# Delta-rule heads of a hybrid transformer block: triangular inverse carried as a product and its transpose, decay rows from DRAM, part of the head work on GpSimd, one load per weight panel

## What is computed

```python
y = silu(dwconv3(x_qkv)); q, k = l2norm(q), l2norm(k)
g = -exp(a_log) * softplus(alpha + dt_bias); beta = sigmoid(b)
gc = cumsum(g) within the chunk
decay = where(i >= j, exp(gc_i - gc_j), 0)
A = where(i > j, (k*beta) k^T * decay, 0)
u, w = solve(I + A, [v*beta, k*beta*exp(gc)])       # unit lower triangular
intra = (q k^T) * decay
for each chunk: v_new = u - w s
                o = (q*exp(gc)) s + intra v_new
                s = s*exp(gc_last) + (k*exp(gc_last-gc))^T v_new
o = rmsnorm(o_forward + o_backward) * silu(gate)
```

## Time and profile before

| | us |
|---|---|
| time, median of 3 runs | 3935.17 (3930.39 to 3940.33) |
| the profiled execution's own time | 3934.58 |
| its span, first to last instruction | 3932.8 |
| PE busy | 3615.5 (92% of the span) |
| DVE busy | 1921.5 (49%) |
| ACT busy | 1653.6 (42%) |
| POOL busy | 48.2 (1%) |
| mean granted TensorE clock | 0.952 |
| the 16 heads' stretches, from one head's table copy (L1171) to the next | 1075.95 in sum |

### The profile page before, as it was taken

How to read it: one execution, slowest core, us unless ns; L and a number is a source line. 1 busy time by engine, 2 the same in 40 slices (tenths; PEclk the granted TensorE clock), 3 DMA queues, 4 the chain that set the end, 5 groups by cost and what they waited for, 6 DMA issues and landing times. The chain is left out here.

```text
span 3932.8 us, 52482 instructions
## 1 busy us (share of the span) xinstructions
PE 3615.5 (92%) x19276; PEld 2985.8 (76%) x19276; DVE 1921.5 (49%) x3357; ACT 1653.6 (42%) x2516; POOL 48.2 (1%) x47
## 2 busy tenths in 40 slices
PE   5999989999989989999999989999889898889899
PEld 4778767777777657877788867777777777659898
DVE  4434446566643444434433344444566664446555
ACT  5323345545543443223422343333454544444444
POOL 0000000000000000000000000000000000000000
PEclk8999989899999989999999999998899999889999
DMA  5433320001012004222422333342010102115454
GB/s 189 139 128 128 139 75 33 32 21 35 30 43 94 13 11 150 97 91 92 138 97 97 106 128 128 139 139 97 33 33 31 38 27 75 65 33 181 150 175 157
DMA packets 93243, 354.94 MB, mean 90 GB/s; under 512 B 5536, under 2 KB 6816, under 8 KB 92992
## 3 DMA queue, kind: packets, MB, share of 16 engines
q1 hardware_dynamic: 93072, 353.11, 26.3%
q0 software_dynamic: 48, 0.13, 0.0%
HBM read 352.17 MB, written 1.05 MB: 90 GB/s over the span
## 5 line engine op out<-in xcount | busy, mean ns | idle before, releaser
L893 DVE TENSOR_TENSOR wlo<-raw,whi 128x1024 fp32r<-128x1024 f32 x664 | 812.3, 1232 | 883.3 <-ACT whi L409 880.6
L409 ACT ACTIVATE whi<-raw 128x1024 fp32r<-128x1024 f32 x664 | 692.9, 1055 | 1251.0 <-PE bank L1499 1099.8
L1499 PE MATMUL bank<-uh,whi 128*128 128x512 f32 (+1 forms) x3008 | 1120.1, 372 | 94.9 <-DVE ul L950 37.0
L1499 PE MATMUL bank<-uh,wlo 128*128 128x512 f32 (+1 forms) x3008 | 1090.7, 363 | 0.5 <-DVE scr L1255 0.4
L1499 PE MATMUL bank<-ul,whi 128*128 128x512 f32 (+1 forms) x3008 | 1087.9, 362 | 0.0
L1499 PEld LDWEIGHTS bank<-uh,whi 128*128 128x128 f32 x3008 | 581.8, 193 | 196.2 <-issue 47.5
L1499 PEld LDWEIGHTS bank<-uh,wlo 128*128 128x128 f32 x3008 | 581.4, 193 | 83.5 <-DVE scr L1255 1.9
L1499 PEld LDWEIGHTS bank<-ul,whi 128*128 128x128 f32 x3008 | 583.4, 194 | 71.2 <-issue 1.4
L1499 PE MATMUL bank<-bh,whi 128*128 128x512 f32 (+1 forms) x1088 | 386.7, 355 | 1.1 <-DVE h L977 0.8
L1499 PE MATMUL bank<-bh,wlo 128*128 128x512 f32 (+1 forms) x1088 | 384.4, 353 | 0.0
L1499 PE MATMUL bank<-bl,whi 128*128 128x512 f32 (+1 forms) x1088 | 384.4, 353 | 0.0
(11 more groups left out here) (223 smaller groups left out, 3940.3 us busy)
## 6 DMA issues: line engine op xcount, KB each, us to landing
raw<-stream SPq DMA_DIRECT2D x332, 1024.0 KB, 4.9
h<-h_in SPq DMA_DIRECT2D x1, 2048.0 KB, 15.2
cst<-consts SPq DMA_DIRECT2D x1, 1281.0 KB, 5.6
out<-m SPq DMA_DIRECT2D x8, 128.0 KB, 1.8
vec<-vecs SPq DMA_DIRECT2D x1, 299.0 KB, 5.9
m<-wab SPq DMA_DIRECT2D x1, 128.0 KB, 14.9
m<-wab POOLq DMA_DIRECT2D x1, 128.0 KB, 2.5
row_vectors<-rows SPq DMA_DIRECT2D x1, 64.0 KB, 10.2
```

The lines of the kernel that those rows point to most:

```text
L409: act.activation(whi[:, j, :], raw[:, j, :], ACT.Copy).then_inc(hi_ready, 1)
L893: dve.tensor_tensor(wlo[:, j, :], raw[:, j, :], whi[:, j, :].bitcast(f32), ALU.subtract).then_inc(lo_ready, 1)
L1499: last = mm(bank[j][:, c0:T], w(t, a), x[:, t, c0:T], start=n == 0, stop=n == 3 * kts - 1)
```

## The change

1. The inverse: the kernel carries Q = A X and its transpose in PSUM (banks 7, 6 and 4, 5) through seven levels, v = 0 to 6. A level is two groups of four matmuls per direction, both of the same pair of operands, `Pm` (masked Q) and the copied transpose; DVE masks one bank into `Pm` while ACT copies the other. A is turned on PE (`a_turned`) for the exact product at the end. `product`, `add`, the identity accumulations and the turn of X go; the finish becomes one float32 product and one float32r product for each direction.
2. The decay rows: for each layer the cumulated decays are turned once, stored to DRAM (`gcd`, 64 rows) and for each head a DMA on ACT's queue broadcasts 4 KB to all 128 partitions (`gcr`, 512 KB). The 8 matmuls per head go. DVE's decay matrix moves into the previous head's finish and state.
3. POOL takes Qt, IT and the output's low part; ACT takes the first convolution tap and the copy of v; ACT's gate input and exponentials move ahead of the output. Splits and preparation have new places in the levels.
4. SP loads each panel by itself (512 KB, four semaphores). The small weight's reload moves from POOL's queue to ACT's.

```diff
@@ SP
+            def load(b, j):
+                sp.dma_start(raw[:, j:j + 1, :], stream[ds(4 * b + j, 1), :, :]...).then_inc(raw_in[j], 16)
             with sp.Fori(1, NB) as b:
-                for r in range(2):
-                    sp.wait_ge(lo_ready, 4 * (b - 1) + 2 * r + 2)
-                    load(b, r)
+                for j in range(4):
+                    sp.wait_ge(lo_ready, 4 * (b - 1) + j + 1)
+                    load(b, j)
@@ POOL, heads(l), for each head
+                    pool.wait_ge(E["qn_ready"], o + 1)
+                    for d in range(2):
+                        pool.wait_ge(E["eg_ready"], 2 * o + d + 1)
+                        pool.tensor_tensor(Qt[:, d, c0:T], qkv[:, 0, c0:T], eg[:, d, c0:T], ALU.mult)...
+                    pool.wait_ge(E["kq_ready"], o + 1)
+                    for d in range(2): ... pool.tensor_tensor(IT[:, d, c0:T], KQs[:, c0:T], DT[:, d, c0:T], ALU.mult)
+                    pool.wait_ge(E["bh_ready"], o + 1)
+                    pool.tensor_tensor(bl[...], gate[:, c0:T], bh[...], ALU.subtract).then_inc(E["head_ready"], 1)
@@ ACT, head(l, b, follow)
+                for v in range(7):
                     for d in range(2):
                         if v < 6:
+                            act.wait_ge(E["q_sum"], 14 * o + 2 * v + d + 1)
+                            act.activation(XT[:, d, :], bank[4 + d][:, :], ACT.Copy).then_inc(E["qtr_ready"], 1)
+                        else:
+                            act.wait_ge(E["qi_sum"], 2 * o + d + 1)
+                            act.activation(X[:, d, :], bank[7 - d][:, :], ACT.Copy, scale=-1.0)...
+                        if follow and (v, d) == (0, 1): prep_in 0, prep_tap 0
+                        if follow and (v, d) == (1, 0): prep_in 1
+                        if follow and (v, d) == (1, 1): load_rows, prep_tap 1
+                        if (v, d) == (2, 0): split(B, 3)
+                        if (v, d) == (2, 1): gate silu
+                        if follow and (v, d) == (3, 0): prep_silu 0
+                        if (v, d) == (3, 1): split(B + 1, 0)
+                        if follow and (v, d) == (4, 0): prep_silu 1
+                        if follow and (v, d) == (4, 1): prep_in 2, prep_tap 2
                         if (v, d) == (5, 0): split(B + 1, 1)
                 if follow:
                     prep_rsqrt(l, b, 0)
                     prep_rsqrt(l, b, 1)
+                    decays(l, b)
+                    gate_in(l, b)
                 output_and_front(l, b, True, follow)
@@ DVE, head(l, b, follow)
                 for v in range(1, 7):
                     for d in range(2):
+                        dve.wait_ge(E["q_sum"], 14 * o + 2 * (v - 1) + d + 1)
+                        dve.tensor_tensor(c4d(Pm[:, d, :]), c4d(bank[7 - d][:, :]), mask, ALU.mult)...
+                        if follow and (v, d) == (2, 0): prep_conv 0
+                        if (v, d) == (2, 1): split(B, 3)
+                        if follow and (v, d) == (3, 0): prep_conv 1
                         if (v, d) == (4, 0): split(B + 1, 0)
+                        if follow and (v, d) == (5, 0): prep_conv 2
                         if (v, d) == (5, 1): split(B + 1, 1)
+                for d in range(2):
+                    dve.wait_ge(E["q_sum"], 14 * o + 12 + d + 1)
+                    dve.tensor_tensor(XT, ident, bank[4 + d], ALU.subtract).then_inc(E["xt_ready"], 1)
+                if follow: decay(l, b, 0)
+                for d in range(2): lx_sum -> dve.tensor_tensor(Pm, bank[4 + d], ident, ALU.subtract) -> sm_ready
                 if follow: prep_var(l, b)
+                for d in range(2): xf_sum -> dve.tensor_tensor(XTf, XT, bank[7 - d], ALU.subtract) -> xf_ready
...
+                    if follow and s == 0:
+                        decay(l, b, 1)
@@ PE, output_and_front
-                    for d in range(2):
-                        for c in range(TC):
-                            last = mm(bank[4 + d][:, sl(c)], hb[:, hcol(HB_G, d, c)].broadcast_to([128, 128]), ...)
-                        last.then_inc(E["gc_row"], 1)
+                gram, k turned, project(8), k times q, project(16)
+                for d in range(2):
+                    pe.wait_ge(E["at_ready"], 2 * f + d + 1)
+                    for c in range(TC):
+                        last = pe.transpose(bank[7 if d == 0 else 2][:, sl(c)], AT[:, d, sl(c)], ident)
+                    last.then_inc(E["a_turned"], 1)
+                    project(12)
@@ PE, head(l, b, follow)
+                def level(v, d):
+                    pe.wait_ge(E["pm_ready"], 14 * o + 2 * v + d + 1)
+                    q, qt = bank[7 - d], bank[4 + d]
+                    ... x = ATr if v == 0 else XT (after qtr_ready of level v-1)
+                    for c in range(TC): mm(qt[:, sl(c)], Pm[:, d, sl(c)], x[:, d, sl(c)], ...)
+                    for c in range(TC): last = mm(q[:, sl(c)], x[:, d, sl(c)], Pm[:, d, sl(c)], ...)
+                    last.then_inc(E["q_sum"], 1)
+                    if v == 6: mm(q[:, :], nidr[:, :], bc(idr[:, :], TC, 128), ...).then_inc(E["qi_sum"], 1)
+                for v in range(7):
+                    fill = 3 if v < 4 else 0
+                    level(v, 0); project(fill); level(v, 1); project(fill)
+                for d in range(2): lmat x XT in float32 (4 matmuls) -> lx_sum
+                project(3)
+                for d in range(2): X x Pm in float32r (4 matmuls) -> xf_sum
+                project(3)
```

More of the change, by code:

```diff
@@ L384, in _, with squares @@
         def _(pool):
-            for n in range(3 * DEPTH + 1):
+            def squares(n):
                 c0 = norm_conds(n)
@@ L630, in output_and_front @@
                 if front:
-                    decay(0)
+                    act.wait_ge(E["v_turned"], f + 1)
+                    act.activation(vtok, bank[2][:, :], ACT.Copy).then_inc(E["vtok_ready"], 1)
+                    act.wait_ge(E["k_turned"], f + 1)
+                    act.activation(ktok, bank[5][:, :], ACT.Copy).then_inc(E["ktok_ready"], 1)
                 if output:
@@ L645, in output_and_front @@
                                    ACT.Copy).then_inc(E["bh_ready"], 1)
-                if not front:
-                    return
-                low_a(0)
-                act.wait_ge(E["gram"], 2 * f + 2)
-                act.activation(KQs[:, c0:T], bank[2][:, c0:T], ACT.Copy).then_inc(E["kq_ready"], 1)
-                x_first(0)
-                low_a(1)
-                if output:
-                    have(act, E["head_ready"], o + 1)
-                gate_in(l, b)
-                x_first(1)
             def head(l, b, follow):
@@ L718, in heads @@
                     prep_rsqrt(l, 0, n)
+                decays(l, 0)
+                gate_in(l, 0)
                 output_and_front(l, 0, False, True)
@@ L1202, in head @@
+                if front:
+                    first_level(1)
+                if output:
+                    dve.wait_ge(E["eo_ready"], o + 1)
+                    dve.tensor_tensor(gate[:, c0:T], gate[:, c0:T], eo[:, 0, c0:T], ALU.mult).then_inc(E["on_ready"], 1)
             def head(l, b, follow):
-                c0 = CTX if l == DEPTH - 1 else 0
                 B = P[("head", l)][0] + b
                 o = l * DNH + b - 1
+                if follow:
+                    prep_vec(l, b)
@@ L1280, in heads @@
                 prep_var(l, 0)
+                for d in range(2):
+                    decay(l, 0, d)
                 output_and_front(l, 0, False, True)
@@ L1690, in output_and_front @@
                 for c in range(TC):
-                    last = pe.transpose(bank[1][:, sl(c)], qkv[:, 1, sl(c)], ident)
-                last.then_inc(E["kv_turned"], 1)
-                project(6)
-                if output:
-                    pe.wait_ge(E["on_var"], o + 1)
-                for c in range(TC):
-                    last = mm(bank[7][:, sl(c)], qkv[:, 1, sl(c)], qkv[:, 1, sl(c)], start=True, stop=True)
-                last.then_inc(E["gram"], 1)
-                project(18)
@@ new lines, in output_and_front @@
+                last.then_inc(E["gram"], 1)
+                for c in range(TC):
+                    last = pe.transpose(bank[5][:, sl(c)], qkv[:, 1, sl(c)], ident)
+                last.then_inc(E["k_turned"], 1)
+                project(8)
+                pe.wait_ge(E["qn_ready"], f + 1)
+                have(pe, pair_done[1], G0 + b + 1)
+                for c in cs:
+                    last = mm(bank[3][:, sl(c)], qkv[:, 1, sl(c)], qkv[:, 0, sl(c)], start=True, stop=True)
+                last.then_inc(E["kq_sum"], 1)
@@ new lines, in output_and_front @@
+                project(16)
+                for d in range(2):
+                    pe.wait_ge(E["at_ready"], 2 * f + d + 1)
+                    if d == 0 and output:
+                        pe.wait_ge(E["on_var"], o + 1)
+                    if d == 1:
+                        pe.wait_ge(E["vtok_ready"], f + 1)
```

(20 more changed lines are left out.)

358 lines of the change are left out of this document (180 added, 178 removed).

## The result

The changed kernel took 3900.09 us (median of 4 runs, 3896.7 to 3901.01) against 3932.78 of the kernel before (4 runs, 3927.75 to 3940.33): 0.9921 of its time, 95% interval 0.9902 to 0.9941. It is 32.7 us faster, less than half of the 71 that were forecast. The value lies in the wide range given (3810 to 3922), outside the forecast's own (3840 to 3885), and nearest to the rival in which the clock takes the gain back (3906). The profiled execution took 3900.23, its span is 3898.4 and its mean granted clock 0.930, where that of before was 0.952.

The account below looks back on a forecast made before the run. PE was taken as the engine without slack. From 3934.58: -36.4 and -27.3 for the two layers' heads, -9 last heads, -6 loads, +8 clock, giving 3864; own range 3840 to 3885, 8 in 10 between 3810 and 3922.

Parts of the forecast that it names:

- the front: Head's front, layer 0: decay rows and XT's turns and copies removed, turns of A and a stall added; -1.5 us, to 17.8.
- the finish: Head's finish, layer 0: turns, residual and last product removed (4.3 us), 2.5 added, PE stopped for some 0.6; -1.2 us.
- the state: Head's state, layer 0: four more DVE operations ahead of the first state copies; +0.2 us, between -0.7 and +1.1.
- The new wait ahead of the output's mean square: Front, layer 0: gate_in ahead of the output's square on ACT waits for panel 3; PE stalls 0.9 us.
- The four waits in the levels: Layer 0 levels: PE stalls ahead of (3,0) 1.5, (3,1) 0.5, (4,1) 2.0 and (5,1) 3.4; 7.4 us together.
- I add 0.6 a head, +8: Heads' levels: a longer stretch without fills, with waits of 2 to 3 us, lowers PE's granted clock; +8 us in all.
- the rival of the clock: All heads: every head falls to the 71.16 us kind at a lower clock; 42 us more, 3906; chance 0.20.
- Single-panel loads: Three places where PE waits for the first panel behind a modulation-weight block: load starts 1.7 us earlier; -6 us.
- the slower rival: Middle of the levels: ACT's DMA issue holds its queue beyond 0.5 us; 3927 at 4.99, 3948 at 6.5; chance 0.07.
- POOL: costed at 0: Qt and IT on POOL in the front: contention with DVE costed at 0, at most 1 us on PE's path.
- First fronts: Each layer's first front: decay rows' store and load lie beside ACT's silus and table load; 0, between -2 and +4.
- last heads: Last head of each layer, without preparation: about -5 each, less the output's slower low part on POOL; -9 for both.

Follow-up runs that it names:

- e2_order: Changed kernel with only DVE's list reordered: three splits' steps and convolution 2, four in all, each one mask later; 3745.67 us, 0.9536 of the kernel before.
- e7_fill_order: Changed kernel with DVE's four steps one mask later and 18 projections a head moved from the front into levels 4 to 6; 3693.81 us, 0.9398 of before.
- e5_single: Kernel before the change with single-panel loads (512 KB, four semaphores) and nothing else; 3905.57 us, 0.9948 of before.
- e6_all: Changed kernel with DVE's steps later, 18 projections moved into levels 4 to 6, and POOL's list reordered (IT, output's low part, Qt); 3694.85 us, 0.9395 of before.

## Why the prediction missed

**Direction, place and cover: right.** The windows show the front at 18.15 against 17.8, the finish at 4.75 against 4.8, the state at 12.88 against 12.8. The new wait ahead of the output's mean square is 0.83 us, forecast 0.9. In the timeline of PE, kernel after:

```profile
924.38 1.13 PE L1736 MATMUL bank<-m,cst 128*128 128x512 f32 x2 [0.83 <-ACT m L679]
```

**The four waits in the levels: right in kind, a little long.** The stops of the head at 853.06 are 0.29, 0.68, 0.20, 1.99 and 2.78 us, each ended by a mask, ahead of levels (2,1), (3,0), (3,1), (4,1) and (5,1): 5.9 against 7.4. The chains are those of the prediction. In the timeline of DVE, kernel after, both long stops stand as a wait for ACT, once for the high part of a split and once for the first tap of convolution 2:

```profile
886.89 1.22 DVE L943 TENSOR_TENSOR wlo<-raw,whi 128x1024 fp32r<-128x1024 f32 x1 [2.25 <-ACT whi L435]
...
891.95 0.75 DVE L1165 SCALAR_TENSOR_TENSOR scr<-scr,hv 128x512 f32<-128x512 f32 x1 [2.64 <-ACT scr L622]
```

The longest were forecast as 2.0 and 3.4 and are 1.99 and 2.78; the ones ahead of (3,0) and (3,1), 1.5 and 0.5, came as 0.68 and 0.20. The 0.29 ahead of (2,1) was not forecast.

**The step that failed: the clock.** The prediction put it at "I add 0.6 a head, +8", and held against the rival of the clock that "groups of 128 columns are not the part that a lower clock hurts". Both are wrong. Such a group costs 0.85 us at the lower clock and 0.45 at the full one. The levels of after were forecast as 20.2 of work and 7.4 of stops and are 26.60 and 5.93: 6.4 us more busy time, 1.5 less stop. Of the 6.4, 5.1 are clock by e2_order; the other 1.3 are in its 21.49 at full clock too, so that the sum of the pieces was short by them. In layer 1 the busy time is some 7 us over the work as e7_fill_order weighs it. Measured over the heads' windows: a clock of 0.89 in 476.68 us and of 0.83 in 455.96 makes 105 + 155 = 260 us at the lower level, where 0.95 in 487.42 and 0.96 in 450.03 made 49 + 36 = 85 before. Each of those 175 us more loses half of itself where PE has work, 87 us at most. The heads fell short of their forecast by 64 - 8 - 4.8 = 51.

The rows on record could have shown it. The prediction added up 22.3 us of work for the levels of before and called the other 8 waits and switches. (Its own pieces, 34 x 0.44 + 24 x 0.23 + 1.7, make 22.2.) But the earlier trace rows say that PE was busy for 26.30 of the 30.35: only 4 of the 8 are stops, and the other 4 are busy time that the sum of the pieces does not explain. The clock beside it is 0.94, some 3.6 us at the lower level, which can account for half of itself, 1.8 of the 4. In the trace of before the group at 910.69 has its successor at 911.51, 0.82 behind it, in that same stretch. The head of 71.16 us beside the one of 68.23 says it as well: its 2.9 us are all busy time (66.32 against 63.38), clock and not the noise that they were taken for. And the reference for 0.6 a head was the difference of two heads of before (0.93 against 0.97, 3 us), in which a clock as low as in the new kernel's heads (0.84 in the one at 3006.53) did not occur; it was no upper bound. The rival of the clock had the right place, and 3906 is 6 us from the result; but it met it by two errors that cancel, since the loads gave 14 us more than the 6 it had from the forecast, and the clock took more than its 42.

**Single-panel loads: right place, too small.** 6 forecast, 20 measured. The sum counted three stops of the kind of the earlier trace rows, and its 1.7 us for each make 5, not 6. The table of stretches puts 8.9 us ahead of the heads and 19.8 between the two layers' heads in the profiled executions, half of it in many small stops and half in busy time, as told with e5_single. The Trainium skill (DMA: Bandwidth & Descriptors, Rules for kernel authors) asks for at least 1 MiB in a DMA; here halving the load to 512 KB made the kernel faster. A panel lands in 3.3 us where a pair took 4.9, and it no longer waits for its pair's split; which of the two did it wasn't tried apart. Nothing in the run shows a loss of bandwidth: between the two layers' heads the DMA engines moved 96 GB/s before and 97 with the half loads.

**The DMA issue on ACT: the slower rival fell.** The timeline of ACT, kernel after:

```profile
877.23 0.34 ACTq L627 DMA_DIRECT2D gc_row<-gc_rows  x1
```

The issue takes 0.34 us, not 5. The 4.99 of the earlier trace rows was an issue at the program's start and no bound for this one. The page gives 3.6 us from the issue to the landing, with some 25 us to go before its use.

**POOL: costed at 0, and 0 as far as e6_all tells,** though its place was misread: an in-order list was read by what each operation needs and not by what stands ahead of it. The prediction also thought the move a loss only beside the masks. POOL did land beside them, and they kept their 0.69, with one operand from PSUM; the taps, with both from SBUF, are what it slowed.

**First fronts and last heads.** The stretch ahead of the heads is 5.7 us longer than with the loads alone, outside the -2 to +4 given; the two longest stops of PE around the start of the first front are 7.88 and 5.30 us where those of before are 5.05 and 4.06. In layer 1 they are 7.58 and 5.31 where they were 4.84 and 3.76, so that by these stops the two first fronts cost some 8 us. The prediction looked at ACT's wait for the store of the decay rows. The timeline of ACT shows none: the load of the rows is issued at 569.13, beside the last tap (569.12 to 569.84), and the next operation starts at 569.86. What lies longer on the path there is the three taps that ACT now makes ahead of the silus, and the two decay matrices on DVE (2.19 us at 579.05) ahead of the operation that ends the second stop; that these are the whole cause wasn't tried. The last heads fell by 4.6 and 4.2 us up to their last state product, the 9 that were forecast for both.

**The whole sum.** Of the 71 us forecast, the heads fell short by 51 and the first fronts by 8, and the loads gave 23 more by the profiled executions (29 for 6). That leaves 35, and the two profiled executions differ by 34.

## What to carry to other kernels

When a sum of pieces falls short of PE's busy time in a stretch, look at the granted clock of that stretch before calling the rest waits: at the lower level the groups of small matmuls too cost nearly twice their time (0.85 us for 0.45 here). In a stretch of short dependent steps it is not enough to remove work; where the work removed was what kept the engine going, spread independent matmuls over the stretch and give each in-order helper engine its own work behind, not ahead of, the step that PE waits for. Here the same instructions in another order gave 206 us, six times the change itself.

## What was not expected of the hardware

- Adding 18 matmuls of 512 columns to each head with a successor didn't make the kernel slower (0.9895 against 0.9921 of before), made the fourteen heads shorter in sum (914.07 us against 932.64), and took their clock from 0.89 and 0.83 in the two layers to 0.94 in both.
- Two neighbouring heads of one execution, with the same instructions and the same first long stop of 1.99 us, took 64.65 and 68.48 us, with clocks of 0.95 and 0.88.
- A tap on DVE (128 x 512, all operands in SBUF) took 1.66 us instead of 0.75 beside a POOL multiplication; the low split in the earlier trace rows, beside one for 0.39 us, had gone from 1.22 to 1.47. A mask, whose one operand comes from PSUM, kept its 0.69 beside the same POOL operations.
- A DMA of one 4 KB row to all 128 partitions, 512 KB written, landed in 3.6 us, nearly as fast as a plain load of 512 KB (3.3), and its issue held ACT's queue for 0.34 us.
